# Feed-forward units of a two-block transformer kernel: high and low halves of the input side by side, one product of 512 columns

## The reference

```
h = x * (1 + sc2) + sh2
a, b = split(h @ w13)        # w13: 1024 x 2*2816
f = (silu(a) * b) @ w2       # w2: 2816 x 1024
x = layer_norm(ALPHA * x + (1 + g2) * f)
...
sh1, sc1, g1, sh2, sc2, g2 = split(silu(c) @ ada_w[1] + ada_b[1], 6)   # next layer
```

## Time and profile before

| | us |
|---|---|
| median of 3 runs | 2277.76 (2276.63 to 2279.03) |
| the profiled execution | 2278.82 |
| its span | 2277.1 |
| PE busy | 2196.4 (96%) |
| DVE busy | 1720.0 (76%) |
| ACT busy | 1374.5 (60%) |
| mean granted TensorE clock | 0.99 |

### The profile page before, as it was taken

One profiled execution on the slowest core, in us unless ns is written; L12 is line 12 of the kernel. 1 busy time (PEld: TensorE's weight loads), 2 busy tenths in 40 slices (PEclk: granted clock), 3 DMA queues, 4 the chain that ended last, 5 costly groups with the idle time before them and its releaser, 6 DMA issues.

```text
span 2277.1 us, 36311 instructions
## 1 busy us (share of the span) xinstructions
PE 2196.4 (96%) x14646; PEld 1884.5 (83%) x14646; DVE 1720.0 (76%) x1680; ACT 1374.5 (60%) x1284; POOL 88.4 (4%) x164
## 2 busy tenths in 40 slices
PE   7999999998999999999999999999998898999998
PEld 5778999986788888888888888888997797788887
DVE  3876444656788888888988888885677377899966
ACT  3244434545677777777777777773565334777754
POOL 7400000001000000000000000000000000000000
PEclk9999999999899999999999999999999899999999
DMA  9786754776499999999999999996841142899960
GB/s 333 234 270 206 259 180 156 235 229 203 163 341 393 381 370 370 372 370 372 369 371 371 370 371 372 367 375 114 212 133 39 54 152 74 331 370 375 368 223 19
DMA packets 339967, 618.78 MB, mean 272 GB/s; under 512 B 24813, under 2 KB 165944, under 8 KB 339800
## 3 DMA queue, kind: packets, MB, share of 16 engines
q1 hardware_dynamic: 338992, 616.13, 77.5%
q10 hardware_dynamic: 808, 0.30, 0.1%
HBM read 614.26 MB, written 1.05 MB: 270 GB/s over the span
## 4 chain that ended last, share of the span: by engine, by line
PE 91%; DVE 4%; ACT 2%; DMA 1%; issue 1%; SPq 0%; DVEq 0%; ACTq 0%
PE bank L1281 12%; PE bank L1282 11%; PE bank L1283 11%; PE bank L2200 6%; PE bank L1314 6%; PE bank L1315 6%; PE bank L1313 6%; PE bank L2202 6%; PE bank L2201 6%; PE bank L2258 2%; PE bank L1254 2%; PE bank L1291 1%; PE bank L2314 1%; PE bank L600 1%; PE bank L1348 1%; PE bank L2396 1%
## 5 line engine op out<-in xcount | busy, mean ns | idle before, releaser
L1400 DVE TENSOR_TENSOR ring_lo<-ring_raw,ring_hi 128x2048 fp32r<-128x2048 f32 x432 | 988.3, 2291 | 138.6 <-ACT ring_hi L1393 138.2
L1393 ACT ACTIVATE ring_hi<-ring_raw 128x2048 fp32r<-128x2048 f32 x432 | 828.0, 1920 | 296.9 <-PE bank L1283 180.6
L1281 PE MATMUL bank<-ring_hi,xg_hi 128*128 128x512 f32 x1152 | 457.1, 397 | 4.0 <-DVE xg_lo L1595 2.1
L1282 PE MATMUL bank<-ring_hi,xg_lo 128*128 128x512 f32 x1152 | 450.2, 391 | 0.0
L1283 PE MATMUL bank<-ring_lo,xg_hi 128*128 128x512 f32 x1152 | 449.9, 391 | 0.0
L476 DVE TENSOR_TENSOR ring_lo<-ring_raw,ring_hi 128x2048 fp32r<-128x2048 f32 (+1 forms) x96 | 218.0, 2280 | 113.1 <-ACT ring_hi L458 104.9
L2200 PE MATMUL bank<-Hh,ring_hi 128*128 128x256 f32 x936 | 267.1, 285 | 4.0 <-issue 2.1
L2202 PE MATMUL bank<-Hh,ring_lo 128*128 128x256 f32 x936 | 265.6, 284 | 0.0
L1281 PEld LDWEIGHTS bank<-ring_hi,xg_hi 128*128 128x128 f32 x1152 | 216.8, 188 | 49.7 <-ACT xg_hi L1457 2.8
L2201 PE MATMUL bank<-Hl,ring_hi 128*128 128x256 f32 x904 | 256.4, 284 | 0.0
L1283 PEld LDWEIGHTS bank<-ring_lo,xg_hi 128*128 128x128 f32 x1152 | 216.7, 188 | 46.9
(11 more groups left out here) (512 smaller groups left out, 2838.4 us busy)
## 6 DMA issues: line engine op xcount, KB each, us to landing
ring_raw<-in_moe_w SPq DMA_DIRECT2D x672, 512.0 KB, 5.2
ring_raw<-in_ada_w SPq DMA_DIRECT2D x96, 512.0 KB, 5.4
ring_raw<-in_ffn_w SPq DMA_DIRECT2D x66, 512.0 KB, 5.1
ring_raw<-in_exp_gate SPq DMA_DIRECT2D x64, 512.0 KB, 4.6
ring_raw<-in_exp_up SPq DMA_DIRECT2D x64, 512.0 KB, 4.7
ring_raw<-in_exp_down SPq DMA_DIRECT2D x64, 512.0 KB, 4.7
ring_raw<-in_w_in SPq DMA_DIRECT2D x42, 512.0 KB, 5.6
ring_raw<-in_conv_in_w SPq DMA_DIRECT2D x16, 512.0 KB, 8.4
```

Of the source, the lines that this page charges most:

```text
L1281: mm(o, xg_hi[:, g, kk, :], wh(k), start=(kk == 0), stop=False)
L1282: mm(o, xg_lo[:, g, kk, :], wh(k), start=False, stop=False)
L1393: nc.scalar.activation(ring_hi[:, at % SPLIT, :], ring_raw[:, n % RAW, :], ACT.Copy)\
L1400: nc.vector.tensor_tensor(ring_lo[:, at % SPLIT, :], ring_raw[:, n % RAW, :], ring_hi[:, at % SPLIT, :].bitcast(F32), ALU.subtract).then_i ...
```

## The change

`Hh` and `Hl` become the two halves of one tensor `Hboth`. In steps 1 to 10 the units a and b go through a new function `stacked`. For each slice and block it issues one product of 512 columns, wh times (Hh | Hl), and one of 256 columns, wl times Hh, into the left half of the same bank. A block now fills a bank, so a unit takes two. The left half holds wh·Hh + wl·Hh, the right half wh·Hl. VectorE copies the left half out (128x256) and adds the right half (128x256), twice per unit; Silu then runs in `tB`, and f is made from two SBUF operands. Step 0 stays as it was.

Each step now takes four of the four rotating banks. Two things are moved: all 4 late adaptive units now stand behind down 0 (before: 3, and 1 behind down 1), and `biased("turn 1 0")` is done in step 2 ahead of `split_lo` (before: step 3, behind it). The diff below follows the order of the program: unit list, tensors, TensorE, ScalarE, VectorE.

```diff
     def down(j):
         add(("ffn2", j), w2, 0, D, 2, r0=256 * j)
-        for _ in range(3):
+        for _ in range(4):
...
-        Hh, Hl = sb("Hh", [P, KT, S], F32R), sb("Hl", [P, KT, S], F32R)
+        Hboth = sb("Hboth", [P, 2, KT, S], F32R)
+        Hh, Hl = Hboth[:, 0, :, :], Hboth[:, 1, :, :]
...
+            def stacked(key, job):
+                n = at_unit[key]
+                banks = [take(pe, f"{job}.{blk}") for blk in range(2)]
+                ready(n)
+                wh, wl = weights(n)
+                for blk in range(2):
+                    o, cs = banks[blk], slice(blk * P, (blk + 1) * P)
+                    both = o[:, :].rearrange("p (i t) -> p i t", i=2)
+                    for k in range(KT):
+                        mm(both, wh[:, k, cs], Hboth[:, :, k, :], start=(k == 0), stop=False, skip_group_check=True)
+                        last = mm(o[:, 0:S], wl[:, k, cs], Hh[:, k, :], start=False, stop=(k == KT - 1),
+                                  skip_group_check=True)
+                    if blk == 0:
+                        last.then_inc(pe.tick(f"mm {job}.0"), 1)
+                unit_end(last, n, f"{job}.1")
...
             for j in range(NP):
                 if j:
-                    columns(("ffn a", j), f"ffn a {j}", Hh, Hl)
+                    stacked(("ffn a", j), f"ffn a {j}")
...
+                    stacked(("ffn b", j), f"ffn b {j}")
                     ffn_down(j - 1)
...
-                    act.eng.wait_ge(*T.at(f"mm ffn a {j}"))
...
+                    if j:
+                        act.eng.wait_ge(*T.at(f"sum ffn a {j}"))
+                        run(tB[:, g:g + 2, :], tB[:, g:g + 2, :], ACT.Silu).then_inc(act.tick(f"gate ffn {j}"), 1)
...
+                    if j == 2:
+                        biased("turn 1 0", [(1, 0)])
                     split_lo(dve, at_unit[("ffn b", j)] + 2)
-                    if j == 3:
-                        biased("turn 1 0", [(1, 0)])
...
+                    def sums(job, dst):
+                        for i in range(2):
+                            b = ps(f"{job}.{i}")
+                            dve.eng.wait_ge(*T.at(f"mm {job}.{i}"))
+                            nc.vector.tensor_copy(dst[:, g + i, :], b[:, 0:S]).then_inc(dve.tick(), 1)
+                            dve.eng.wait_ge(*dve.own())
+                            tt(dst[:, g + i, :], dst[:, g + i, :], b[:, S:2 * S], ALU.add)\
+                                .then_inc(dve.tick(f"ev {job}.{i}"), 1)
+                            T.mark(f"sum {job}", *dve.last)
+
+                    if j:
+                        sums(f"ffn a {j}", tB)
+                        sums(f"ffn b {j}", tC)
+                        dve.eng.wait_ge(*T.at(f"gate ffn {j}"))
+                        dve.eng.wait_ge(*dve.own())
+                        tt(tC[:, g:g + 2, :], tB[:, g:g + 2, :], tC[:, g:g + 2, :], ALU.mult).then_inc(dve.tick(), 1)
```

More of the change, by code:

```diff
@@ L2459, in _ @@
                         turn_row(lambda l, p: b3[:, 4 * p:4 * p + 4])
-                columns(("ffn b", j), f"ffn b {j}", Hh, Hl)
                 if j:
+                    stacked(("ffn b", j), f"ffn b {j}")
                     ffn_down(j - 1)
+                else:
+                    columns(("ffn b", j), f"ffn b {j}", Hh, Hl)
             ffn_down(NP - 1)
@@ L2746, in _ @@
                     split_hi(act, at_unit[("ffn b", j)] + 2)
-                    act.eng.wait_ge(*T.at(f"mm ffn a {j}"))
[L2748 to L2752, removed]
+                    g = 2 * (j % 4)
+                    if j:
+                        act.eng.wait_ge(*T.at(f"sum ffn a {j}"))
+                        run(tB[:, g:g + 2, :], tB[:, g:g + 2, :], ACT.Silu).then_inc(act.tick(f"gate ffn {j}"), 1)
+                    else:
+                        act.eng.wait_ge(*T.at(f"mm ffn a {j}"))
+                        run(tB[:, g:g + 2, :], ps(f"ffn a {j}")[:, :].rearrange("p (k t) -> p k t", k=2), ACT.Silu)\
+                            .then_inc(act.tick(f"ev ffn a {j}"), 1)
+                        T.mark(f"gate ffn {j}", *act.last)
                     act.eng.wait_ge(*T.at(f"f ffn {j}"))
@@ L3133, in _ @@
                 if j < NP:
+                    if j == 2:
+                        biased("turn 1 0", [(1, 0)])
                     split_lo(dve, at_unit[("ffn b", j)] + 2)
-                    if j == 3:
-                        biased("turn 1 0", [(1, 0)])
[L3137 to L3141, removed]
-                    g = 2 * (j % 4)
-                    tt(tC[:, g:g + 2, :], tB[:, g:g + 2, :],
-                                ps(f"ffn b {j}")[:, :].rearrange("p (k t) -> p k t", k=2), ALU.mult).then_inc(dve.tick(f"ev ffn b {j}"), 1)
+                    g = 2 * (j % 4)
+                    def sums(job, dst):
[13 more added lines that the diff above has]
+                        tt(tC[:, g:g + 2, :], tB[:, g:g + 2, :], tC[:, g:g + 2, :], ALU.mult).then_inc(dve.tick(), 1)
+                    else:
+                        dve.eng.wait_ge(*T.at(f"mm ffn b {j}"))
+                        dve.eng.wait_ge(*T.at(f"gate ffn {j}"))
+                        tt(tC[:, g:g + 2, :], tB[:, g:g + 2, :],
+                           ps(f"ffn b {j}")[:, :].rearrange("p (k t) -> p k t", k=2), ALU.mult)\
+                            .then_inc(dve.tick(f"ev ffn b {j}"), 1)
                     T.mark(f"f ffn {j}", *dve.last)
```

## The result

| | before | after |
|---|---|---|
| median, us | 2278.88 of 20 runs (2276.63 to 2280.54) | 2283.74 of 20 runs (2280.80 to 2290.75) |
| the profiled execution, us | 2278.82 | 2283.95 |
| its span, us | 2277.1 | 2282.2 |

The ratio is 1.0025, 95% interval 1.0019 to 1.0031, which is +5.7 us (4.3 to 7.1); the two medians differ by 4.9. The forecast was +2.5. The kernel became slower, by about the 0.2% (4.6 us) from which on the prediction counted a difference. The 20 runs of before have a median of 2278.88, 1.1 us over that of the three runs on which the forecast stood, so 1.1 us of the distance between 2280.3 (forecast) and 2283.74 is that of the starting point.

What follows compares the result with a forecast made beforehand. TensorE's list of products plus its waits bounds the stage. From 2278.82 us, -3.8 (products) +4.7 (wait) +1.7 (clock), VectorE's work hidden, gives 2281.4, or 2280.3 as a median; range 2276.8 to 2284.4.

Steps and rivals of the forecast that it cites:

- What bounds the kernel: Feed-forward stage: as long as TensorE's list of products plus whatever TensorE is made to wait.
- The products: Units a and b, steps 1 to 10: 320 pairs each save 0.012 us (0.360 to 0.348), gain 3.8 us.
- rival 3: Stacked products: two-piece operand, Hh/Hl copy or size change costs a product's start; pair stays 0.360, gain 0, 2284.1 us; chance 0.09.
- Rival 2: Stacked products: 512 columns cost 0.234 us as in the first mixture; gain 1.9, time 2282.2 us; chance 0.20.
- VectorE's added work: Feed-forward steps: copies and additions, 3.4 us a step, hidden beside TensorE; cost nothing, 1.6 us left at the last step.
- The wait: Late adaptive work before a2: chain through ScalarE, TensorE, VectorE starts a2 at 10.2 us, 4.7 us more than 5.5.
- The clock: Start of a2: 1.2 GHz for some 3.6 us after the wait, 1.7 us lost; bounds 0 and 2.4.
- The sum: Whole kernel: 2278.82 - 3.8 + 4.7 + 1.7 = 2281.4 us profiled, 2280.3 median, 2.5 us over 2277.76.
- The chances: Whole kernel's time: 0.69 within 0.2% (4.6 us), 0.26 slower by more, 0.05 faster by more.

Runs made afterwards that it cites:

- one_piece: Changed kernel whose 512-column products read 512 adjoining values instead of two pieces 8 KB apart, low half of input left out: 2286.41 us, single run.
- copies_three: Changed kernel with a2's halves made ahead of the waits, plus each of VectorE's four copies a step done three times: 2284.26 us, single run.
- fillers: Changed kernel with 16 and 18 unused dense products of 128 columns in TensorE's two waits: 2283.24 us against 2279.59 before, ratio 1.0017.
- fillers_short: Changed kernel with 8 and 10 unused dense products of 128 columns in TensorE's two waits: 2280.85 us against 2279.01 before, ratio 1.0011.
- grouped: Changed kernel with the 8 wide products of each block first, then its 8 narrow ones: 2281.75 us, single run.
- move_only: Kernel before with only the two moves of adaptive work and no stacked products: 2287.74 us against 2279.59, ratio 1.0033.

## Why the prediction failed, step by step

- **What bounds the kernel:** held. The stage is TensorE's list plus its waits, before and after.
- **The products, 3.8 us:** too large, it is 2.3. The step that failed is "I take 0.228, because those products share the two-piece read with the new ones": the pair was put at 0.348 us and takes 0.353 in nine steps of ten. The read has no part in it (one_piece). Those rows have only products of one size, and with the sizes in groups the pair is at 0.349 to 0.350. So the change between 512 and 256 columns, which rival 3 listed at 12 ns a pair, is a likely reason at 4 ns, but step 2 alternates at 0.347, and why is open. Rival 2 had the size, 0.354 a pair, with the price of another place. With the 2.3 the forecast would have been 1.5 us higher. (Rival 3's "from 0.353 a pair on" is a slip: by its own sum 2282.3 is passed from 0.354 on.)
- **VectorE's added work, nothing:** held. Copies and additions take 0.42 us, TensorE waits for none of them, and copies_three found the margin of the last step.
- **The wait, 4.7 us:** held. 10.37 us against 10.2, 4.84 more than before; the order of three in-order engines gave it link by link.
- **The clock, 1.7 us:** the fall was foreseen, at half; its length was not. It is 4.75 us of a2 and not 3.6, so 2.2 us; fillers has 2.2 and fillers_short 2.0. The failed step is the 3.6, read at a place where dense products had followed on one-column ones. The upper bound of that step, 2.4 us, held it; its 5.2 us is 5.0 by the rows (602.13 + 4.45 to 611.6), so the bound should have been 2.3.
- **The sum:** the corrected terms give +4.7 us where I had +2.6. The stage has +4.48. The whole runs have +4.9 by their medians and +5.7 (4.3 to 7.1) by the ratio, whose lower part agrees. Some 1 us beyond the terms stays open. It may be nothing, or the later clock dips: those between 516 and 618 us and from 1744 on start and last differently in the traces of the kernels, in code that no run here edits, and no run separates them from the change. The median of 2283.74 lies inside the range that I gave, by luck: its upper end was rival 3's, with no gain from the products at all.
- **The chances:** 0.69 stood on "within 0.2%", because +2.5 lay well inside 4.6 us. The two errors, 1.5 and 0.5 us, point the same way and took it up to that bound; the open 1 us lies beyond it, and the interval of the ratio (from 4.3 on) holds both sides. 0.26 had been left for "slower".

The Trainium skill's rule ("TensorE: Matmul & The Clock Gate", section "Back-to-back issue gap"), which it gives for the isolated gap and by which joining two products saves 2.5 ns, would give 0.8 us. The traces have 6.7 ns a pair as built in nine steps, 13 ns in step 2 and some 10.5 ns grouped, so its size does not agree.

## What to carry to other kernels

Joining two products of 256 columns into one of 512 saved 7 ns a pair as built, and 10 ns in every step once equal sizes were issued together; why alternating pairs ran at two paces is open, so read the pace of each unit and not one mean. When work is moved on one engine, follow it on every in-order engine that serves it. Here a unit of 0.9 us that moved, with its turnings, cost 4.8 us of wait, because two splits that the next unit needed now stood behind instructions that wait; a split issued ahead of the wait took all of it back. And price a gap on TensorE with its clock: here two gaps of together 4.7 us cost 2.2 us more.

## What the runs showed of the hardware that I had not expected

- Alternating 512 and 256 columns, a wide product took 0.236 us and a narrow one 0.117 (0.353 together) in most steps, but the same pair took 0.347 in step 2 of four of the six kernels with that order; in groups of eight of one size, 0.230 and 0.120 (0.350) in all steps. A moving operand in two pieces 8 KB apart made no difference (0.3533 a pair against 0.3534).
- A single gap of 2.1 us on TensorE, between dense products, was followed by 3.4 us at 1.2 GHz (copies_three), where 3 us with 1.66 us of products had kept 2.4 GHz.
- In the same stretch the clock fell at different places in different executions: in grouped it was at half from 236.0 on, before the second turning, while in the changed kernel it fell at 238.3, behind it.
- The changed kernel's 20 runs scatter by 10 us, the 20 of before beside them by 4. That this comes with the change is not shown, since the 22 runs of before beside move_only scatter by 8. The changed kernel's fastest run (2280.80) had a mean granted clock of 0.989, the slowest (2290.75) 0.984.
